# An even mixer reordered: head norms beside its own query, key and value tiles, memory projection tiles between the attention steps

## The reference, cut to what matters

```python
def even_mixer(h, positions, w_in, q_gain, k_gain, w_s, b_s, ln_g, ln_b, w_out):
    q, k, v, pu, pv = split(h @ w_in)                 # five parts of 512 columns
    q = partial_rope(rmsnorm(heads(q), q_gain), positions)      # 8 heads of 64
    k = partial_rope(rmsnorm(heads(k), k_gain), positions)
    a = moba_attention(q, k, heads(v))                # 256 tokens: causal attention
    u, vg = gelu(pu), gelu(pv)
    g = chunked_spatial_gating(u, vg, w_s, b_s, ln_g, ln_b)     # needs vg normalised
    return concat([a, g]) @ w_out

def mem_cross_attention(x, mem_n, w_q, w_kv, ...):    # follows the mixer
    k, v = split(mem_n @ w_kv)                        # 256 memory rows, 2048 columns
    ...
```

## Time and profile before

| | us |
|---|---|
| median of 3 runs | 1709.52 (1707.77 to 1711.32) |
| the profiled execution's own time | 1702.04 |
| its span in the profile | 1700.3 |
| PE busy, PE weight loads busy | 1604.6, 1523.9 |
| DVE busy, ACT busy | 1128.2, 807.7 |
| mean granted clock of PE | 0.97 |

### The profile page before, as it was taken

One profiled execution on the slowest core, in us unless ns is written; L12 is line 12 of the kernel. 1 busy time (PEld: TensorE's weight loads), 2 busy tenths in 40 slices (PEclk: granted clock), 3 DMA queues, 4 the chain that ended last, 5 costly groups with the idle time before them and its releaser, 6 DMA issues.

```text
span 1700.3 us, 31460 instructions
## 1 busy us (share of the span) xinstructions
PE 1604.6 (94%) x12572; PEld 1523.9 (90%) x12572; DVE 1128.2 (66%) x2032; ACT 807.7 (48%) x1402; POOL 188.7 (11%) x200
## 2 busy tenths in 40 slices
PE   6988999999998899999998989999989999899998
PEld 5876898999997699999996688999989999899997
DVE  5884644777675667777677755666677566566666
ACT  4446225444354554445554455544455555554443
POOL 2670501000031020002000011000020002010000
PEclk9998898999999999999998799999999999999999
DMA  6420002454553045544542142555535444256552
GB/s 212 148 81 20 1 2 96 152 180 166 183 189 132 1 149 199 197 171 176 194 153 99 50 150 80 169 199 198 171 114 188 141 158 152 75 171 199 186 174 88
DMA packets 125813, 236.56 MB, mean 139 GB/s; under 512 B 2614, under 2 KB 50025, under 8 KB 125689
## 3 DMA queue, kind: packets, MB, share of 16 engines
q1 hardware_dynamic: 124393, 230.29, 39.2%
q0 software_dynamic: 1296, 4.53, 0.8%
HBM read 233.76 MB, written 1.05 MB: 138 GB/s over the span
## 4 chain that ended last, share of the span: by engine, by line
PE 83%; DVE 10%; ACT 3%; issue 2%; SPq 0%; DMA 0%; POOL 0%; DVEq 0%; ACTq 0%; POOLq 0%
PE ps L602 46%; PE ps L649 6%; PE ps L648 6%; PE ps L647 6%; PE ps L610 5%; DVE w_lo L1927 3%; PE ps L780 3%; PE ps L741 2%; PE ps L698 2%; PE ps L929 1%; PE ps L754 1%; PE ps L911 1%; DVE u_lo L1947 1%; DVE hidden L1978 1%; ACT w_hi L1406 1%
## 5 line engine op out<-in xcount | busy, mean ns | idle before, releaser
L1406 ACT ACTIVATE w_hi<-raw 128x1024 fp32r<-128x1024 f32 x440 | 460.2, 1051 | 291.8 <-PE ps L649 137.3
L1927 DVE TENSOR_TENSOR w_lo<-raw,w_hi 128x1024 fp32r<-128x1024 f32 x440 | 540.7, 1229 | 10.4 <-ACT w_hi L1406 10.2
L602 PE MATMUL ps<-u_hi,w_hi 128*128 128x256 f32 (+1 forms) x1544 | 446.9, 289 | 14.9 <-DVE u_lo L1947 8.6
L602 PE MATMUL ps<-u_hi,w_lo 128*128 128x256 f32 (+1 forms) x1544 | 440.8, 285 | 0.0
L602 PE MATMUL ps<-u_lo,w_hi 128*128 128x256 f32 (+1 forms) x1544 | 440.4, 285 | 0.0
L602 PEld LDWEIGHTS ps<-u_hi,w_hi 128*128 128x128 f32 x1544 | 294.4, 191 | 21.6 <-DVE u_lo L1947 10.6
L602 PEld LDWEIGHTS ps<-u_hi,w_lo 128*128 128x128 f32 x1544 | 294.8, 191 | 0.0
L602 PEld LDWEIGHTS ps<-u_lo,w_hi 128*128 128x128 f32 x1544 | 293.8, 190 | 0.5
L602 PE MATMUL ps<-a_hi,w_hi 128*128 128x256 f32 (+1 forms) x800 | 230.0, 288 | 5.3 <-DVE a_lo L1942 2.3
L602 PE MATMUL ps<-a_lo,w_hi 128*128 128x256 f32 (+1 forms) x800 | 227.2, 284 | 0.0
L602 PE MATMUL ps<-a_hi,w_lo 128*128 128x256 f32 (+1 forms) x800 | 227.1, 284 | 0.0
(11 more groups left out here) (377 smaller groups left out, 2359.6 us busy)
## 6 DMA issues: line engine op xcount, KB each, us to landing
raw<-in_w_ff_dram SPq DMA_DIRECT2D x32, 2048.0 KB, 8.5
raw<-in_ffn_w_gu_dram SPq DMA_DIRECT2D x44, 1024.0 KB, 7.5
raw<-in_ffn_w_down_dram SPq DMA_DIRECT2D x10, 2048.0 KB, 7.8
raw<-in_xa_w_kv_dram SPq DMA_DIRECT2D x8, 2048.0 KB, 8.0
raw<-in_od_w_in_dram SPq DMA_DIRECT2D x6, 2048.0 KB, 8.0
raw<-in_w_in_ab_dram SPq DMA_DIRECT2D x5, 2048.0 KB, 7.8
raw<-in_ev_w_in_dram SPq DMA_DIRECT2D x5, 2048.0 KB, 8.1
raw<-in_xa_w_q_dram SPq DMA_DIRECT2D x4, 2048.0 KB, 7.8
```

The lines of the kernel that those rows point to most:

```text
L602: mm = pe.matmul(bank[:, 0:n], wx[:, q, k * P:(k + 1) * P], x[ux][:, k, ts], start=k == 0 and i == 0, stop=k == KD - 1 and i == 2)
L1406: act.activation(quarter(w_hi, b, q), raw_quarter(b, q), ACT.Copy).then_inc(high_split, 1)
L1927: dve.tensor_tensor(quarter(w_lo, b, q), raw_quarter(b, q), quarter(w_hi, b, q).bitcast(F32), ALU.subtract)\
```

## The change

The five blocks of `ev_in` are reordered to `gu`, `gv`, query, key, value. The gate blocks come first, as plain blocks, with their GELU on ACT behind them. The memory operand, the angle chain, the sines and the transposes of the mixing weights follow directly. Two query tiles precede the head norms, and the other ten tiles of query, key and value lie between the head-norm units. All 16 memory tiles move into the attention, one per step in steps 0 to 15, on PE, ACT and DVE alike; the hook's old work (`gate_step`) comes first in each step on ACT and DVE. PE's spatial gating moves to step 17. The causal units now use the banks, waits and lag of the `window` kind (`beside_tiles`). The attention's results go to `u`, since `a` holds the memory operand until the last memory tile. The diff, cut to its core:

```diff
-            add("ev_in", [[cols(w["ev_w_in_2"][0], c)] for c in range(0, 2560, BLOCK)], token_blocks=(2, 4))
+            add("ev_in", [[cols(w["ev_w_in_2"][0], c)] for c in (1536, 2048, 0, 512, 1024)], token_blocks=(1, 4))
...
-            bank = b7 if near(x) else tile_bank[1 + v % 3]
+            bank = b7 if beside_tiles(x) else tile_bank[1 + v % 3]
...
+        def beside_tiles(x):
+            return near(x) or x["kind"] == "causal"
...
-            return b6 if near(x) else (b6, b7)[v % 2]
+            return b6 if beside_tiles(x) else (b6, b7)[v % 2]
...
-            return 4 + 3 * i // 2, 4 + 3 * (i + 1) // 2
+            return 2 + 10 * i // 8, 2 + 10 * (i + 1) // 8
...
                 def values(i):
-                    if near(x):
+                    if beside_tiles(x):
                         if i >= 1:
                             pe.wait_ge(operand_split, split0 + i)
                     elif i >= 3:
                         pe.wait_ge(operand_split, split0 + i - 2)
...
# PE
-                    block_t(b + 1, u, REAL)
-                    block_v(b + 2, u, NMETA)
-                    block_t(b + 3, u, REAL)
-                    block_v(b + 4, u, NMETA)
+                    block_v(b + 1, u, NMETA)
+                    turn_mixing_weights()
+                    def mixer_tiles(lo, hi):
+                        for n in range(lo, hi):
+                            i, t = 2 + n // 4, n % 4
+                            if i == 4:
+                                tile_v(b + i, t, u, NMETA)
+                            else:
+                                tile_t(b + i, t, u, REAL)
+                    mixer_tiles(0, 2)
+                    pe.wait_ge(M["ws_read"], 2)
+                    head_norms([(1, SEQ, blk64)] * 8, table("swap_halves"), between=lambda i: mixer_tiles(*ev_fill(i)))
...
-                    turn_mixing_weights()
-                    memory_tiles(0, 4)
-                    pe.wait_ge(M["ws_read"], 2)
-                    head_norms([(1, SEQ, blk64)] * 8, table("swap_halves"), between=lambda i: memory_tiles(*ev_fill(i)))
                     pe.wait_ge(hn_roped, ropes[0])
+                    pe.wait_ge(tile_read, tile_at[first_of("xkv0")])
+                    def memory_step(k):
+                        if k < 16:
+                            memory_tiles(k, k + 1)
+                        if k == 17:
+                            pe.wait_ge(at_exp, at[0] + 16)
+                            spatial_gating()
...
-                    attention(units, "mix_out0")
+                    attention(units, None, between=memory_step)
+                    u, a = a, u
...
# ACT
                     stream("ev_in", gelu, 0, 2)
                     memory_operand()
-                    stream("ev_in", gelu, 2)
                     ...
-                    memory_tiles(0, 4)
-                    head_norms(..., between=lambda i: memory_tiles(*ev_fill(i)))
+                    mixer_tiles(0, 2)
+                    head_norms(..., between=lambda i: mixer_tiles(*ev_fill(i)))
+                    normed, product = product, normed
                     def gate_norm(k):
+                        gate_step(k)
+                        if k < 16:
+                            memory_tiles(k, k + 1)
...
# DVE
-                lag = 5 if near(units[0]) else 6
+                lag = 5 if beside_tiles(units[0]) else 6
...
+                    def mixer_tiles(lo, hi):
+                        for n in range(lo, hi):
+                            i, t = 2 + n // 4, n % 4
+                            b = phases["ev_in"].first + i
+                            project_ev(i, t, tile_at[b] + t)
+                            split_low(b + 1, t - 1)
                     stream("ev_in", project_ev, 0, 2)
                     memory_low()
-                    stream("ev_in", project_ev, 2)
                     ...
-                    memory_tiles(0, 4)
+                    mixer_tiles(0, 2)
                     dve.wait_ge(M["rope_sin"], 1)
-                    head_norms(..., between=lambda i: memory_tiles(*ev_fill(i)))
+                    head_norms(..., between=lambda i: mixer_tiles(*ev_fill(i)))
+                    normed, product = product, normed
...
                     def gate_norm(k):
+                        gate_step(k)
+                        if k < 16:
+                            memory_tiles(k, k + 1)
```

More of the change, by code:

```diff
@@ L1354, in _ @@
                                 keys=[(P, c * P, [mv[:, c, 64 * h:64 * h + 64]]) for c in range(m + 1)]))
-                    attention(units, "mix_out0")
+                    attention(units, None, between=memory_step)
+                    u, a = a, u
                     ready = [op[0] - 6 + 2 * k for k in range(4)]
-                    spatial_gating()
                     op[0] += 2
@@ L1800, in gelu @@
                     def gelu(i, t):
-                        if i == 3:
+                        if i == 0:
                             act.wait_ge(tile_read, first + 4 * i + t + 1)
                             act.activation(gu[:, t], gu[:, t], ACT.Gelu).then_inc(M["gelu"], 1)
-                        if i == 4:
+                        if i == 1:
                             act.wait_ge(tile_read, first + 4 * i + t + 1)
@@ L1807, in gelu @@
                             act.activation(part, part, ACT.Gelu).then_inc(M["gelu"], 1)
+                    def mixer_tiles(lo, hi):
+                        for n in range(lo, hi):
+                            split_high(phases["ev_in"].first + 2 + n // 4 + 1, n % 4)
                     stream("ev_in", gelu, 0, 2)
                     memory_operand()
-                    stream("ev_in", gelu, 2)
                     act.wait_ge(M["rope_angle"], 1)
@@ L1816, in _, with gate_step @@
                     log_and_exp()
-                    memory_tiles(0, 4)
-                    head_norms([(x[:, i], SEQ, 1.0 / 64, SEQ, (tile_read, first + 4 * j + i + 1))
+                    mixer_tiles(0, 2)
+                    head_norms([(x[:, i], SEQ, 1.0 / 64, SEQ, (tile_read, first + 8 + 4 * j + i + 1))
                                 for j, x in enumerate((mq, mk)) for i in range(4)],
-                               between=lambda i: memory_tiles(*ev_fill(i)))
+                               between=lambda i: mixer_tiles(*ev_fill(i)))
+                    normed, product = product, normed
                     def gate_norm(k):
+                        gate_step(k)
+                        if k < 16:
+                            memory_tiles(k, k + 1)
+                    def gate_step(k):
                         if k == 5:
@@ L2554, in project_ev, with mixer_tiles @@
                             turn_rs(rs_tok[:, 0:2], 2)
-                        if i in (2, 4):
-                            part = (mv, gv)[i // 4][:, t % 2, t // 2 * HALF:(t // 2 + 1) * HALF]
+                        if i in (1, 4):
+                            part = (gv, mv)[i // 4][:, t % 2, t // 2 * HALF:(t // 2 + 1) * HALF]
                             scaled_tokens(part, t, gt, rs_tok[:, t % 2:t % 2 + 1])
                         else:
-                            scaled((mq, mk, None, gu)[i][:, t], t, gt, REAL)
+                            scaled((gu, None, mq, mk)[i][:, t], t, gt, REAL)
+                    def mixer_tiles(lo, hi):
+                        for n in range(lo, hi):
+                            i, t = 2 + n // 4, n % 4
+                            b = phases["ev_in"].first + i
+                            project_ev(i, t, tile_at[b] + t)
+                            split_low(b + 1, t - 1)
                     stream("ev_in", project_ev, 0, 2)
                     memory_low()
-                    stream("ev_in", project_ev, 2)
                     dve.wait_ge(late_in, 16 * N_LATE_LOADS)
@@ L2582, in _ @@
                             .then_inc(M["ws_read"], 1)
-                    memory_tiles(0, 4)
+                    mixer_tiles(0, 2)
                     dve.wait_ge(M["rope_sin"], 1)
                     head_norms([([x[:, i]], [col(g)], [x[:, i]]) for x, g in ((mq, "ev_q"), (mk, "ev_k")) for i in range(4)],
-                               rope=[(cos_m, sin_m)] * 8, between=lambda i: memory_tiles(*ev_fill(i)))
+                               rope=[(cos_m, sin_m)] * 8, between=lambda i: mixer_tiles(*ev_fill(i)))
+                    normed, product = product, normed
                     zeros_at = C["zeros"][0]
```

## The result

The changed kernel takes 1735.62 us (median of 4 runs, 1732.32 to 1740.91) against 1708.64 us before; the ratio is 1.0154, 95% interval 1.0129 to 1.0179. The forecast was 1724, range 1707 to 1733. The direction and the place of the waits were right; the loss is 27 us where 14.5 was forecast.

The account below looks back on a forecast made before the run. PE was taken as the bound, busy 1604.6 of 1700.3 us. Stages gave +0.9 to the eighth tile, +8.3 for the norms' idle start, attention 94.9 in place of 42.7: 1709.5 + 14.5 = 1724 us, range 1707 to 1733.

Parts of the forecast that it names:

- Stage 1: Gate blocks, first to eighth projection tile: GELU table and GELUs before the splits cost 1.1 us, between 0 and 3.
- Stage 2: Eighth tile to first norm: operand and angle chain leave PE idle about 8.7 us; first scaling at 844.8.
- The restart: PE's first work after its idleness before the norms: some 3.5 us at 1.2 GHz, a loss of 1.7 us.
- Stage 3: Head norms with ten tiles instead of twelve: 36.5 us; attention starts at 885.0, against 922.7.
- Stage 4: Attention with 16 memory tiles, to the end of tile 15: 62.7 us of work plus 16.0 of waits, 78.7.
- 62.7 us of PE's own work: Attention to tile 15 at full clock: 16 tiles at 3.04, scores 7.4, transposes 2.5, values 4.2.
- The wait that the change creates: Attention lockstep: PE's values await a low part DVE writes behind the tile's read-out; 14.2 plus 1.8 us, 16.0 together.
- Rival (c): Attention: clock falls, half the steps with a hole run at 1.2 GHz, 5 tiles x 2.84 us; 1738, chance 0.06.
- Stage 5: Tail after tile 15: five more units through one bank, to the output tile's read-out; 16.2 us, bounds 13 and 20.
- (a): Attention: the lockstep doesn't bite, DVE runs ahead; without the 16.0 us the time is 1708, no change; chance 0.08.
- (b): Norms and attention: lockstep absent and norms start early, PE's 8.7 and 1.7 us covered too; 1697.6, chance 0.12.
- The signs: Profile: PE idle 8 us before norms, clock 0.50 after, ten low-part waits of 1.3 to 2.4 us; wrong if tiles at 1.2 GHz.

Follow-up runs that it names:

- e1: Changed kernel with DVE writing the low part of unit k-5 before reading memory tile k, not behind it; 1720.1 us, ratio 1.0055.
- e12: Changed kernel with three constant matmuls nobody reads put on PE ahead of the values in steps 6 to 15; 1733.2 us, ratio 1.0127.
- e5: Changed kernel with DVE's angle chain moved ahead of its wait for the layer's norm; 1737.0 us, ratio 1.0158.
- e6: Changed kernel with angle chain, memory operand and the two sines with their tables all ahead of the layer's norm; 1731.6 us, ratio 1.0142.
- e3: Changed kernel with four constant matmuls nobody reads put on PE ahead of the values in steps 6 to 15; 1736.7 us, ratio 1.0145.
- e2: Changed kernel with two places in the result bank, so values wait for the low part of the unit before the last; 1714.6 us, ratio 1.0032.
- e9: Changed kernel with e6, e1, e2, two later ACT splits; two memory tiles before the attention, 14 in steps 3 to 16; 1699.1 us, ratio 0.9940.

## Why the prediction was wrong, by its steps

| stage | forecast, counted from the first tile | measured |
|---|---|---|
| eighth tile read | 22.3 | 23.5 |
| first norm scaling | 39.2 | 40.7 |
| attention's first scores | 79.4 | 81.4 |
| last memory tile's end | 158.1 | 167.9 |
| first output tile read | 174.3 | 188.4 |

A tile's end is put 0.29 us ahead of its read-out here, as the forecast did.

- **Stage 1** was 1.2 us short, and that is the clock and not the splits: the first 3.8 us of the layer ran at 0.66. In e1 and e12, where they ran at 1.00, the eighth tile is read at 22.0, close to the 22.3 of the forecast. In the trace of before they ran at 1.00 too; whether the change brings the lower clock there, no run shows.
- **Stage 2** was right: PE waits 8.4 us where 8.7 was forecast. e5 and e6 show that its cause is the chain operand, angle, sines, tables.
- **The restart** at half clock was right in kind: the first tile takes 4.00 instead of 2.83 and the first sums 1.19 instead of 0.43 to 0.67, together 1.7 to 1.9 where 1.7 was forecast.
- **Stage 3** held within 0.5.
- **Stage 4** is the step that failed, and in it one term: the 62.7 us of PE's own work "at full clock". Up to the end of tile 15 the stage took 86.5 us where 78.7 was forecast. The wait that the change creates was there as described, and was even priced too high: 10.5 us on the low part and 3.1 on ACT's copies, together 13.5, against 16.0. What is left for PE's own work is 73.0 instead of 62.7. Of the 10.3 us between them, 7.0 are tiles (55.7 against 48.6): four that ran at half clock for a part, at 1.5 us each, and the first at 1.3, less 0.4 on two tiles that were quicker. The other 3.2 or so are scores, transposes and values, 17.3 against 14.1; the values of 128 keys, for one, take 0.40 in such a step where 0.29 was taken.
- **Rival (c)**, the falling clock, had a chance of 0.06, on the ground of a single hole of 0.95 us that left the clock alone. Here holes of 1.05 to 1.8 us return in every step from 6 to 15. That their repetition counts, I had no row for and should not have argued from one. e3 and e12 show that filling them restores the clock, e1 and e2 that removing them does, and e12 that this is worth time. (c)'s 1738 is nearer to 1735.6 than the forecast, but by luck: it priced five tiles at 2.84 us more, and four had 1.5.
- **Stage 5** was 4.3 short. 1.2 is again the clock: DVE waits 2.98 for the first output tile where it waited 1.76, with PE restarting after 3.3 us of idleness and a clock of 0.59 from 993 to 997. About 2.2 is PE's order: the spatial gating, priced as lying beside the results, stands in PE's queue between the values of units 12 and 13, so the low parts at 982.63 and 986.28 are 3.65 apart instead of 1.4. That second part is read from the trace and was not tried; the remaining 0.9 is open.
- **Rivals (a) and (b)** are refuted as statements on this kernel. What they describe can be had when more is mended: e2, without the lockstep, is at 1.0032 where (a) had no change, and e9, without it and with an early start of the norms, is at 0.9940 where (b) had 12 us less, 0.993.
- **The signs.** PE's idleness before the norms, the half clock behind it and the ten waits on the low part came as named, though they are 0.6 to 1.4 us long and not 1.3 to 2.4. One of the signs of being wrong came too: memory tiles that run at 1.2 GHz, four of them in part.
- **The range** (1707 to 1733) failed by 2.6 us. The 62.7 had no bound of its own. The upper bounds that the prediction does give (1.9 on stage 1, 1.8 on the restart, 6.0 on the wait, 3.8 on the tail) reach 1737.5 when they are added up; taken together as 1732 they left no room for a term that had none. A range that held 1735.6 in that way would have held it by luck.

## What to carry to other kernels

When tiles are put between the steps of a pipeline, look for the one buffer whose release stands in another engine's queue behind the read-out of the tile just computed: that makes a step the sum of both. Either the other order removes it, or a second place for results, so that only the one before the last has to be awaited. Work that used to lie between two dependent chains was their cover; when it moves, the chains meet. A small hole on PE in every step can cost more than its length, as the clock may go down with it: here 13.5 us of holes brought 6 us of slow tiles. When a trace shows a few tiles of one kind half as long again, read the granted clock and look at the holes ahead of them. And count waits up to the same point to which they were priced: over the whole stage the two kinds come to 18.5 us, which would have hidden that they were priced too high and that PE's own work was priced too low.

## What was not expected of the hardware

Matmuls that nobody reads made PE's stage shorter: with 30 of them in ten steps the clock of the attention is 1.00 from 912 to 978 and 81.1 us replace 87.2. And in e2 PE wrote one unit's result into a PSUM bank while DVE read the one before from the other half of its partitions, in other columns: PE's values at 954.60 last 0.65 us (a modelled end), DVE's read stands at 954.88 and lasts 0.28. The values without a read beside them, at 948.87 and 959.18, last 0.65 as well, so no cost shows.
